# Attention that starts with the prompt and ends with the sample, and value products in groups of four heads

## The reference

```
h = rms_norm(x);  qa, ka, va, qb, kb, vb = split(h @ w_in)      # q and k normed per head, qb and kb rotated
A: 8 heads, a chunk of 64 queries sees its own chunk and 8 before it:
   p = softmax(q k^T * SCALE + bias[head, clipped distance]);  o = p v
B: 8 query heads on 2 key heads, own chunk and 2 before it, with a sink per head:
   p = exp(s - m) / (sum exp(s - m) + exp(sink - m));          o = p v
sample: 64 queries against a cache of 128 keys and its own 64
x = x + concat(A, B) @ w_out;   x = x + conv_ffn(rms_norm(x))
```

## Time and profile before

| | us |
|---|---|
| median of 3 runs (2541.45 to 2551.11) | 2542.08 |
| the profiled execution, and its span | 2547.8, 2545.7 |
| busy in the span: PE, PEld, DVE, ACT, POOL | 2390, 2229, 1726, 1164, 990 |
| from the last PE work of `project` to the first of `attend` | 24.7 |
| `attend`, from its first score to the last value product | 494.9 to 932.6 |
| from there to the first PE work of `combine` | 12.0 |

### The profile page before, as it was taken

How to read it: one execution, slowest core, us unless ns; L and a number is a source line. 1 busy time by engine, 2 the same in 40 slices (tenths; PEclk the granted TensorE clock), 3 DMA queues, 4 the chain that set the end, 5 groups by cost and what they waited for, 6 DMA issues and landing times. The chain is left out here.

```text
span 2545.7 us, 45276 instructions
## 1 busy us (share of the span) xinstructions
PE 2390.3 (94%) x15773; PEld 2228.8 (88%) x15773; DVE 1725.6 (68%) x3746; ACT 1163.7 (46%) x2658; POOL 990.4 (39%) x1150
## 2 busy tenths in 40 slices
PE   7999999588999979998999999999999999999997
PEld 4888888467877869998899999989999998999997
DVE  7667666466766756676676667767766777676765
ACT  6232332376776753325443444543444454444443
POOL 1988888557888878831220000213000021000001
PEclk9999999799999989999999999999999999999999
DMA  8777776656667659889696666969666687666665
GB/s 259 219 224 210 214 224 190 165 143 177 185 171 191 184 178 347 288 299 333 213 306 215 215 214 206 323 231 303 224 210 222 216 270 264 211 215 213 221 207 183
DMA packets 318237, 578.32 MB, mean 227 GB/s; under 512 B 35490, under 2 KB 167826, under 8 KB 317890
## 3 DMA queue, kind: packets, MB, share of 16 engines
q1 hardware_dynamic: 274576, 424.24, 52.5%
q0 software_dynamic: 39872, 149.75, 18.5%
q10 hardware_dynamic: 3570, 1.52, 0.3%
HBM read 444.88 MB, written 132.10 MB: 227 GB/s over the span
## 5 line engine op out<-in xcount | busy, mean ns | idle before, releaser
L2142 PE MATMUL ffn_x<-carry_big 128*128 128x352 f32 x2508 | 458.8, 324 | 13.0 <-PEq L62 5.6
L2142 PEld LDWEIGHTS ffn_x<-carry_big 128*128 128x128 f32 x2508 | 410.7, 189 | 19.3 <-issue 13.2
L2142 PE MATMUL ffn_z<-ffn_h_hi_S,carry_big 128*128 128x352 f32 x1056 | 276.4, 324 | 16.7 <-DVE carry_big L2287 10.3
L316 PE MATMUL project_z<-project_w_hi,project_h_hi 128*128 128x512 f32 (+3 forms) x680 | 256.1, 377 | 18.9 <-DVE project_w_lo L489 15.0
L316 PE MATMUL project_z<-project_w_lo,project_h_hi 128*128 128x512 f32 (+3 forms) x680 | 252.4, 371 | 0.0
L316 PE MATMUL project_z<-project_w_hi,project_h_lo 128*128 128x512 f32 (+3 forms) x680 | 252.3, 371 | 0.0
L2041 POOL TENSOR_TENSOR carry_x<-carry_x,carry_work 128x352 f32<-128x352 f32 x48 | 52.2, 1088 | 503.8 <-DVE carry_work L2405 445.4
L2287 DVE TENSOR_TENSOR carry_big<-carry_w_raw,carry_big 128x512 fp32r<-128x512 f32 (+2 forms) x413 | 224.9, 552 | 0.6 <-ACT carry_big L2223 0.4
L2035 POOL DMA_DIRECT2D carry_work<-h_sums_scratch x8 | 4.4, 554 | 566.9 <-DVE ffn_y_lo_S L2309 562.4
L2142 PEld LDWEIGHTS ffn_z<-ffn_h_hi_S,carry_big 128*128 128x128 f32 x1056 | 186.8, 188 | 22.6 <-DVE carry_big L2287 22.4
L2223 ACT ACTIVATE carry_big<-carry_w_raw 128x512 fp32r<-128x512 f32 (+2 forms) x413 | 195.9, 501 | 5.5 <-PEq L62 4.5
(11 more groups left out here) (265 smaller groups left out, 6506.1 us busy)
## 6 DMA issues: line engine op xcount, KB each, us to landing
carry_big<-t_gu_scratch SPq DMA_DIRECT2D x264, 512.0 KB, 4.1
carry_big<-t_dn_scratch SPq DMA_DIRECT2D x240, 256.0 KB, 3.3
carry_w_raw<-w_gu SPq DMA_DIRECT2D x198, 256.0 KB, 4.2
t_gu_scratch<-project_quads POOLq DMA_DIRECT2D x68, 512.0 KB, 4.5
carry_w_raw<-w_dn SPq DMA_DIRECT2D x180, 128.0 KB, 3.5
project_quads<-w_quads POOLq DMA_DIRECT2D x68, 256.0 KB, 4.6
carry_w_raw<-w_o SPq DMA_DIRECT2D x24, 512.0 KB, 5.7
t_dn_scratch<-attend_quads POOLq DMA_DIRECT2D x22, 512.0 KB, 4.6
```

The source lines that it names most:

```text
L316: last = nc.tensor.matmul(z[c][0:w, 0:width], h[:, k, 0:w], ww[:, k, first:first + width], start=(k == 0 and h is hi and ww is w_hi), stop ...
L2142: mm = nc.tensor.matmul(bank[:, 0:SUB], weights(c)[:, wp, k, :], (hi, lo)[a][name][:, 1 if short else k, :], start=first and k == 0 and (w ...
```

## The change

The diff has four parts.

**Order.** n = 0 to 15 are now prompt tiles 0 to 15, and n = 16 is the sample. The cache goes into key tile 0 and the sample's keys into key tile 1 when these are no longer read. The cache's keys are split in the middle of the stage: ACT at (n, u) = (8, 9), POOL behind `split_b(8)`.

**First operands.** `Passed` holds buffers that outlive `project`. Its SP issues the bias table, its first column and the raw queries and keys of prompt tile 0 in its last turn (`load_attention`), and its DVE subtracts the column from the table. The stores of the last tile are no longer waited for at the barrier, but by SP in `attend` (`last_st`). The activation table load, the loads of identity and cache and several memsets leave the start of `attend`. The sinks are set by DVE at (0, 2).

**Value products.** Four per tile and mixer pair become groups of four heads: 4 a tile, at u = 1, 3 (B, of the tile before) and u = 7, 11 (A), with 256 columns in `o_ps`, six instead of four `prob_t` buffers, and one `invert`, `copy_r` and `divide` for each group.

**Places.** `split_a(n + 1)` moves from u = 8 to u = 7, and the last 3 spots of pieces become 1, so that the last spot has 2 pieces and the first, which was empty, has one.

```diff
+            def load_attention():
+                row = rel_rows.shape[1] * rel_rows.shape[2]
+                sp.wait_ge(rel_st, 16)
+                sp.wait_ge(h_lo_ok, TILES)
+                sp.wait_ge(ssq_ok, TILES)
+                sp.dma_start(passed.bias[:], bass.AP(rel_rows.tensor, P - 1, [[row - 1, P], [rel_rows.shape[2], HEADS], [1, 2 * P]]))\
+                    .then_inc(passed.bias_ld, 16)
+                sp.dma_start(passed.far[:], rel_rows[:, :, 0:2]).then_inc(passed.bias_ld, 16)
+                sp.wait_ge(st_a, 32 * (TILES - 2))
+                sp.wait_ge(st_b, 16 * (TILES - 1))
+                sp.wait_ge(z_ok[VA], TILES - 1)
+                load_raw(sp, passed.raw, q_a, k_a, qk_b, 0, P, passed.raw0_ld)
...
+                if t + 1 == TILES:
+                    load_attention()
                 if t:
                     store_a(t - 1)
...
-            sp.wait_ge(rel_st, 16)
-            sp.wait_ge(st_a, 32 * TILES)
+            sp.wait_ge(st_a, 32 * (TILES - 1))
...
+            dve.wait_ge(passed.bias_ld, 2 * 16)
+            for h in range(HEADS):
+                nc.vector.tensor_scalar(bias[:, h, :], bias[:, h, :], far[:, h, 0:1], None, ALU.subtract)\
+                    .then_inc(passed.bias_sub, 1)
...
-        def product_at(n, u, by=4):
+        def group_at(n, u, by=4):
 
             n, u = before(n, u, by)
-            if n < 0 or (u < A_UNITS and u % 2 == 0):
+            if n < 0 or (u % 4 != 3 if u < A_UNITS else u % 2 == 0):
                 return None
...
             spots = [(n, j) for n in range(1, TILES + 1) for j in range(3) if j == 1 or n >= FULL]
-            spots += [(TILES + 1, j) for j in range(3)]
+            spots += [(TILES + 1, 1)]
...
                 split_b(n)
-            for j in range(3):
-                weights(TILES + 1, j)
+                if n == CACHE_TILE:
+                    pool.wait_ge(cache_hi, 1)
+                    nc.gpsimd.tensor_tensor(keys[low, :, CACHE * P:NEW * P], cache[low, :, :], keys[low, :, CACHE * P:NEW * P].bitcast(F32),
+                                            ALU.subtract).then_inc(cache_lo, 1)
+            weights(TILES + 1, 1)
             prep.stored()
...
+                for a in range(2):
+                    for j in range(w):
+                        for i in range(2):
+                            src = prob_t[(k - 3 + 2 * a + i) % T_BUFS][:, j * P:(j + 1) * P] if g < 2 else \
+                                prob_t[(k - 1 + a) % T_BUFS][:, (i * w + j) * P:(i * w + j + 1) * P]
+                            first = (4 * g + 2 * a + i) * HEAD if g < 2 else PAIRS_A * P + i * HEAD
+                            nc.tensor.matmul(o_ps[i * HEAD:(i + 1) * HEAD, a * P:(a + 1) * P], v[:, tile + j, first:first + HEAD],
+                                             src, start=(j == 0), stop=(j == w - 1))
...
-                if u == 8 and prefetch:
+                if u == 7 and prefetch:
                     split_a(n + 1)
...
+                if (n, u) == (CACHE_TILE, 9):
+                    act.wait_ge(cache_ld, 6 * 16)
+                    act.wait_ge(s_ok, UNITS * FULL)
+                    nc.scalar.activation(keys[:, :, CACHE * P:NEW * P], cache[:], ACT.Copy).then_inc(cache_hi, 1)
```

More of the change, by code:

```diff
@@ L152, with __init__, twice, load_raw @@
 PREPARED = ((0, 68), (68, 110), (110, 132))
-def project(nc, x_tiles, x_rows, w_in, gains, gains_rope, rope_rows, ident, rel, q_a, k_a, qk_b, v_all, rel_rows,
+class Passed:
+    def __init__(self, nc, ctx):
+        m = Memory(nc, ctx, "passed")
+        with ExitStack() as before:
+            self.last_operands = [before.enter_context(nc.sbuf_tensor(f"project_h1_{part}", [P, KD, P], F32R))[:] for part in ("hi", "lo")]
+        self.raw = m.sbuf("raw", [P, HEADS + HEADS + 2, P])
+        self.bias = m.sbuf("bias", [P, HEADS, 2 * P])
+        self.far = m.sbuf("far", [P, HEADS, 2])
+        self.ident = m.sbuf("ident", [P, P])
+        self.raw0_ld, self.bias_ld, self.bias_sub, self.bias_set, self.last_st = (
+            m.sem(n) for n in ("raw0_ld", "bias_ld", "bias_sub", "bias_set", "last_st"))
+def twice(eng, dst, src, sem):
+    for i in range(2):
+        eng.dma_start(dst[i * HEAD:(i + 1) * HEAD], src).then_inc(sem, 16)
+def load_raw(eng, raw, q_a, k_a, qk_b, c, w, sem):
+    by_heads = "f (a p) n -> p (f a) n"
+    twice(eng, raw[:, 0:HEADS, 0:w], q_a[:, :, c:c + w].rearrange(by_heads, p=HEAD), sem)
+    twice(eng, raw[:, HEADS:2 * HEADS, 0:w], k_a[:, :, c:c + w].rearrange(by_heads, p=HEAD), sem)
+    twice(eng, raw[:, 2 * HEADS:, 0:w], qk_b[HEADS // 2:, :, c:c + w].rearrange(by_heads, p=HEAD), sem)
+def project(nc, passed, x_tiles, x_rows, w_in, gains, gains_rope, rope_rows, ident, rel, q_a, k_a, qk_b, v_all, rel_rows,
             prep_range, w_quads, t_gu, t_dn):
@@ L167, in project @@
         m = Memory(nc, ctx, "project")
-        w_hi = m.sbuf("w_hi", [P, KD, COLS], F32R)
-        w_lo = m.sbuf("w_lo", [P, KD, COLS], F32R)
-        pool_mem = m.sbuf("stage", [P, 2944])
-        prep = WeightSums(m, prep_range, w_quads, t_gu, t_dn)
-        x_raw = m.sbuf("x_raw", [P, KD, P])
-        h_hi = [m.sbuf(f"h_hi{i}", [P, KD, P], F32R) for i in range(2)]
-        h_lo = [m.sbuf(f"h_lo{i}", [P, KD, P], F32R) for i in range(2)]
-        x_tok = m.sbuf("x_tok", [P, D_MODEL])
+        operands = [m.sbuf(f"h0_{part}", [P, KD, P], F32R)[:] for part in ("hi", "lo")]
+        h_hi, h_lo = zip(operands, passed.last_operands)
         sq = m.sbuf("sq", [P, HA * HEAD])
@@ L812, in _ @@
                     store(n - 1, 1)
+                if n == CACHE_TILE - 1:
+                    load_cache()
             for n in (TILES - 1, TILES):
@@ L950, in values @@
+                pe.wait_ge(rden_ok, c + 1)
+                for a in range(2):
+                    for i in range(2):
+                        last = nc.tensor.matmul(r_ps[i * HEAD:(i + 1) * HEAD, a * P:(a + 1) * P],
+                                                rden[c % 2][:, 2 * a + i:2 * a + i + 1].broadcast_to([P, HEAD]), ident_sb[:],
+                                                start=True, stop=True)
                 last.then_inc(pv_ok, 1)
-            pe.wait_ge(k0_ok, 2)
+            pe.wait_ge(zero_ok, CLEARED)
@@ L1032, in step @@
                     split_b(n)
-                if u == 8 and prefetch:
+                if u == 7 and prefetch:
                     split_a(n + 1)
-            row = rel_rows.shape[1] * rel_rows.shape[2]
-            nc.scalar.dma_start(bias[:], bass.AP(rel_rows.tensor, P - 1, [[row - 1, P], [rel_rows.shape[2], HEADS], [1, NEAR]]))\
-                .then_inc(bias_ld, 16)
-            nc.scalar.dma_start(far[:], rel_rows[:, :, 0:2]).then_inc(bias_ld, 16)
+                if (n, u) == (CACHE_TILE, 9):
+                    act.wait_ge(cache_ld, 6 * 16)
+                    act.wait_ge(s_ok, UNITS * FULL)
+                    nc.scalar.activation(keys[:, :, CACHE * P:NEW * P], cache[:], ACT.Copy).then_inc(cache_hi, 1)
             nc.scalar.dma_start(sink[:], sinks.rearrange("(a n) -> a n", a=1)).then_inc(sink_ld, 16)
-            for i in range(2):
-                nc.scalar.dma_start(raw[i * HEAD:(i + 1) * HEAD, 0:HEADS, 0:DEC], q_a[:, :, SEQ:].rearrange("f (a p) n -> p (f a) n", p=HEAD)).then_inc(ld, 16)
-            act.wait_ge(cache_ld, 64)
-            for first, count, cache in caches:
-                nc.scalar.activation(keys[:, first:first + count, CACHE * P:NEW * P], cache, ACT.Copy).then_inc(k0_hi, 1)
-            act.wait_ge(zero_ok, 2)
-            act.wait_ge(ld, 7 * 16)
+            act.wait_ge(passed.raw0_ld, 6 * 16)
             split_keys(0)
```

252 lines of the change are left out of this document (116 added, 136 removed).

## The result

The changed kernel takes 2518.34 us (median of 4 runs, 2510.49 to 2523.11), the kernel before beside it 2545.01 (4 runs, 2541.45 to 2551.11). The ratio is 0.9887, with a 95% interval of 0.9868 to 0.9906: 1.1% faster. The forecast was 2511.5 us, 0.9880 of the time that it started from, with a range of 2498 to 2525. The profiled execution took 2519.03 with a span of 2517.2.

What follows compares the result with a forecast made beforehand. Full tiles were taken as paced by a ring through PE, DVE, ACT and POOL, 16.1 + 11.1 us, beside an idle border. Terms summed to -30.6 from the median of 2542.1, giving 2511.5 us, range 2498 to 2525.

Steps and rivals of the forecast that it cites:

- The border, -16.0: From `project` to `attend`: the first score comes at 478.9 instead of 494.91, 16.0 us earlier.
- I cost both at nothing: End of `project`: the added loads and DVE's eight subtractions cost 0; up to 3 us if POOL's last piece is delayed.
- the barrier's 1.2 us: Between `project` and `attend`: 1.2 us left for the barrier itself once the last stores are not awaited.
- Light tiles and sinks, -9.8: Tiles with 1 to 4 key tiles save 11.6 us; setting the sinks at (0, 2) costs 1.8.
- Full tiles, +6.4 at a period of 25.6: Twelve full tiles at 25.6 us, 307.2 in all, against eleven taking 300.8: 6.4 us more.
- The ring: Full tiles: 16.1 us from L861's end to the next keys' low part, shortened to 14.5, plus POOL's 11.1, set the period.
- moving `split_a` to u = 7 costs and gives nothing: Full tiles: splitting the next queries one step earlier is worth 0, since L861 starts when its piece ends.
- POOL paces at 24.9: Rival, full tiles: ACT's keys come even earlier and POOL sets a 24.9 us period; 2503 us, chance 0.10.
- The stall, +11.6 + 2.6: Tiles 8 and 9: POOL's cache split waits for ACT and delays tile 9's keys, 11.6 us; half clock afterwards, 2.6.
- The half clock at tile 9: After PE's idle time of about 12 us, up to 8.7 us at half clock cost up to 2.6; 2.6 taken.
- The sample's tile gone from the start and put at the end, -17.3 - 8.1 = -25.4: Start of `attend` loses the sample's tile, 17.3 us; the end, with that tile, still gets 8.1 us shorter.
- POOL sets the end: End of `attend`: POOL's pieces and last store take 29.0 us, PE's path to the last output 27.6; 8.1 saved.

Runs made afterwards that it cites:

- the joined one: Changed kernel with the cache keys' pass on DVE in two halves and one weight piece moved from the projections to tile 4: 2500.86 us, ratio 0.9833.
- `end_and_first`: Changed kernel with POOL's mixer b queries ahead of its pieces in the sample's tile, and ACT splitting tile 1's keys at u = 7: 2529.01 us, one run.
- `pairs`: Changed kernel with value products of two heads, as in the kernel before, instead of groups of four: 2544.54 us (10 runs), ratio 0.998.

## Why the prediction was nearly right, step by step

By the trace of after, the stretch up to the next stage got 21.4 us shorter, where the sum had 30.6. The other 7.1 us between the two profiles came from behind it.

- **The border, -16.0: measured -11.7.** The step that failed is "I cost both at nothing". It named what it hung on, POOL's last piece, but laid the risk on the new loads and took POOL's last store from one profile, 464.64. In nine profiles since, with as many pieces ahead of it, it was issued between 464.0 and 470.3, in the old projections at 468.1, so the loads are not needed for that. Nor is the barrier's 1.2 us the price behind it: in five profiles, this one among them, the stage began 3.4 us behind the landing of that store. In the other six with the new border it began 1.3 us behind the end of SP's last issue, as forecast with 1.2: at 472.7 to 473.3, the forecast's 473.0, in four (the split back at u = 8, the two kernels with a piece moved, and the joined one), with the first score at 477.4 to 478.0; and at 474.7 and 475.6 in two (`end_and_first`, `pairs`), where the projections themselves ended later. So -11.7 is one draw: the repeated profile of the same kernel had -14.9. In the kernel before, SP's last store held the stage until 475.51 and hid a last store of POOL issued earlier than some 467 to 468. The eight subtractions took 3.24 us, not 2.19, but off the path. What makes POOL late is not settled: its waits for transfers in the projections were 1.7 us before and 2.6 to 7.0 later, in no order that follows its last store (4.6 where it was earliest).
- **Light tiles and sinks, -9.8: measured -7.5.** The sinks took 1.75 us on DVE, as costed. The groups did not: `pairs` gives them 4.8 us, near the lower bound of 4 and not the 9 taken, and 3.5 us are the earlier `split_a`, which stood at nothing. Two costs of tile 0 stood in no term. There is one raw buffer: ACT stands at (0, 5) for 2.80 us until the last transfer for tile 1 has landed, and PE idles 2.40. And the clock stayed at half for 19.9 us from the first score; where it came back after 14.1 to 14.9 us, tile 0 took 1.4 to 2.1 us less (last section).
- **Full tiles, +6.4 at a period of 25.6: measured 307.67 - 299.94 = +7.7 without the stall, mean 25.67.** The ring is the forecast's: 14.4 us to the keys and 11.1 of POOL, with POOL waiting 1.06. Two steps in it were wrong and hid behind the right period. PE would still need 25.1, not 24.2, with POOL out of the way: its own work was right to 0.2 (24.4), but 0.7 us of waits on exponentials stood in no term. And "moving `split_a` to u = 7 costs and gives nothing": at u = 8 PE would wait 1.0 us a tile for the exponentials behind it and pace the tile at 26.0. Both limits lie within a microsecond of the ring. The rival "POOL paces at 24.9" could not have come, since a tile takes 25.1 even with POOL out of the way.
- **The stall, +11.6 + 2.6: measured 37.2 + 27.8 - 2 x 25.5 = 14.0.** POOL's wait for ACT was 8.9 us, not 7; the keys queued behind it and PE's wait of 11.35 came as written. Moved away, it gave back 9.9 to 12.7 us. Its 14 us are 0.55%; without them the rest of the change would by the sum have won some 0.6% beside the groups, where it won 0.1%, and with the pass on DVE it did win 0.4% (0.9858 against 0.9898).
- **The half clock at tile 9.** Tile 9's first two steps took 2.13 and 4.00 us, together 2.2 above the 1.20 and 2.68 of other full tiles. The rows:

```profile
701.80:705.80 4.00, 3.97 (x18) 3.54 (x20) 1.59 (x3) 1.06 (x3) 3.45 (x5) 0.50 0.77 198
705.80:709.80 4.00, 4.00 (x38) 3.69 (x35) 2.15 (x6) 1.79 (x4) 3.72 (x6) 0.73 1.16 247
```

  If the clock is at either level and no other, that is 4 and about 2.2 us at half, and the 2.2 us lost are some 36% of 6.2. In four other profiles with the same stall the clock was at half for 3.1, 3.8, 4.0 and 5.9 us from tile 9's first score, and these two steps took 0.85, 1.09, 1.20 and 2.15 us more: 27 to 36% of the time at half, like the 1.0 for 3.4 of the earlier trace rows. The Trainium skill ("TensorE: Matmul & The Clock Gate", "HAM oscillation — how this bites in real kernels") charges half of the throttled time, and all six measurements here are below that. The forecast's 2.6 was near for this profile; its 8.7 us came from the border and not from a stall.
- **The sample's tile gone from the start and put at the end, -17.3 - 8.1 = -25.4: measured -18.8 - 4.9 = -23.7.** By first maxima the tile took 515.01 - 496.18 = 18.8 at the start, and from the last tile's first maximum to the next stage it was 936.63 - 901.42 = 35.2, now 915.27 - 885.00 = 30.3. The step "POOL sets the end" failed by a little: the last output did, since PE waits 3.27 us for L915 behind two pieces, a queue that the forecast had listed for POOL and not for PE. (The forecast's terms for PE, 17.3, 6 and 4, add up to 27.3 and not to 27.6; nothing hung on it.) A kernel without that wait ended later still, by POOL's store.
- **Behind the stage, 0: the first profile had -7.1.** In eleven profiles with 22 or 23 pieces there, the stretch from the first product to the end was 1592.7 to 1602.0, and 1601.2 in the kernel before; the changed kernel alone had 1594.2 and 1602.0. It is scatter.

The misses, 4.3 + 2.3 + 1.3 + 1.7 less 0.2 on the stall, are 9.4, the difference of 30.6 and 21.4 but for rounding and the choice of marks. That the ratio came within 0.1% of the forecast is in part luck. The medians lie 26.7 us apart and not 30.6, and the time of before that the forecast started from, 2542.08 of three runs, was 2545 to 2548 in the runs since. The first profile reached its time with 21.4 us from the stage and 7.1 of scatter behind it, the repeated one (24.8 us from the stage) with a POOL that came earlier at the border.

## What to carry to other kernels

A stage boundary that waits for several ends hides the scatter of all but the last; before one of them is taken away, look at how far the next moves from run to run, since one profile shows a single draw of it. When an engine paces a ring with a microsecond to spare, a one-time pass queued on it cost nearly its whole length in both places tried here (2.7 of 3.0 us in the better one), and its wait for another engine on top; put it on an engine that idles, ahead of a wait that it has anyway. And where several limits lie within a microsecond (here 25.1 by PE and its waits for exponentials, 25.5 by the ring, 26.0 by ACT's order), test each alone: the right period proves none of the steps.

## What the runs showed of the hardware

A DVE subtraction of two SBUF operands did not run beside a POOL subtraction of SBUF operands, it waited for its end. It took 1.49 us with POOL idle (at 492.02 in the kernel before), 1.49 beside POOL's memsets (at 477.81, above), and 3.33 when it started 1.97 us ahead of the end of a POOL subtraction. Half of it took 0.82 alone and 3.10 when it started 2.42 us ahead of such an end. POOL's own pass that started 0.77 us before DVE's ended took 3.54 in place of 2.91. The Trainium skill ("SBUF — State Buffer", "Who interferes with whom") has it so, for a DVE instruction with two SBUF inputs against a GpSimd one that reads SBUF, and not against one that only writes it; the trace agrees in both.

The clock came back late in the new first tile, and not at the same time in each profile. In the kernel before, the granted clock was 0.50 for 8.7 us from the first score. In the changed kernel it was 0.50 for 19.9 us, from 483.23 to about 503.15; PE was busy for 5.3 of the first 8.7 us and then idled 2.4 in one piece:

```profile
483.23:491.93 8.70, 5.29 (x21) 4.36 (x21) 5.76 (x26) 3.95 (x16) 3.05 (x3) 0.50 1.03 227
495.90:499.90 4.00, 4.00 (x23) 3.69 (x22) 1.55 (x6) 3.06 (x12) 3.92 (x2) 0.50 0.04 5
499.90:503.90 4.00, 4.00 (x31) 3.53 (x30) 1.43 (x5) 2.21 (x11) 3.70 (x6) 0.59 0.58 134
```

The kernel with one piece fewer in the projections has the same code here and the same first 8.7 us, yet its clock was back 14.3 us behind its first score (477.95):

```profile
477.95:486.65 8.70, 5.29 (x21) 4.36 (x21) 5.77 (x26) 3.95 (x16) 3.04 (x3) 0.50 1.04 228
491.95:495.95 4.00, 3.63 (x38) 3.01 (x36) 1.68 (x6) 3.30 (x16) 3.84 (x4) 0.96 0.00 0
```

Over eight profiles with this code in tile 0 the clock was back after 14.1 to 14.9 us in three, where tile 0 took 18.2 to 18.8 us, and after 19.9 to 22.2 in five, where it took 20.2 to 21.1. So some 2 us of tile 0 come and go with the clock under the same code; what sets them is not shown.
